# Attention maps mixed by ScalarE and GpSimd in place of VectorE, and the residual input added by TensorE

## What is computed

```python
q, k, v = split(h @ w_qkv); q = partial_rope(rmsnorm(q)); k = partial_rope(rmsnorm(k))
s = jnp.einsum('mbhqd,mbhkd->mbhqk', q_blk, k) * scale      # two maps m per head
p = jax.nn.softmax(s, axis=-1)
a = p[0] - lam * p[1]
o = jnp.einsum('bhqk,bhkv->bhqv', a, v)
o = rmsnorm(o, sub_gain) * (1.0 - lambda_init)
x = x + o @ w_o
```

## Time and profile before

| | us |
|---|---|
| median of 3 runs | 985.96 (985.76 to 987.13) |
| profiled execution, its own time | 985.77 |
| its span in the trace | 984.0 |
| TensorE busy | 971.3 (99%) |
| VectorE busy | 851.8 (87%) |
| ScalarE busy | 458.5 (47%) |
| GpSimd busy | 354.4 (36%) |

### The profile page before, as it was taken

The page is one execution under the profiler, slowest core; times in us unless marked ns, Lnnn a source line. Parts: engine busy times, 40 slices in busy tenths (PEclk is TensorE's granted clock), DMA queues, the critical chain, the costliest instruction groups (busy, mean ns, idle before and its releaser), DMA issues.

```text
span 984.0 us, 12869 instructions
## 1 busy us (share of the span) xinstructions
PE 971.3 (99%) x4706; PEld 799.2 (81%) x4706; DVE 851.8 (87%) x1132; ACT 458.5 (47%) x703; POOL 354.4 (36%) x317
## 2 busy tenths in 40 slices
PE   8999999989999999999999999999999999999998
PEld 7877778767887888888888888988888888888887
DVE  6696898999688999999989888779998989989883
ACT  5435555656556353443535533475355253452520
POOL 6841454121164638366543100550430403405000
PEclk9999999999999999999999999999999999999999
DMA  7242220120242233332333241303342332422202
GB/s 263 87 107 86 65 68 19 65 108 22 65 171 86 86 114 100 115 100 86 119 95 125 68 158 36 129 1 129 86 128 86 103 111 85 129 86 86 86 1 86
DMA packets 51543, 92.24 MB, mean 94 GB/s; under 512 B 8332, under 2 KB 9368, under 8 KB 51480
## 3 DMA queue, kind: packets, MB, share of 16 engines
q1 hardware_dynamic: 46032, 91.24, 29.0%
q10 hardware_dynamic: 5448, 0.17, 0.3%
HBM read 89.30 MB, written 2.10 MB: 93 GB/s over the span
## 4 chain that ended last, share of the span: by engine, by line
PE 70%; DVE 1%; ACT 0%; issue 0%; DVEq 0%; ACTq 0%
PE pair L1704 35%; PE bank L1704 34%; DVE s_acc L1543 0%; PE bank L2058 0%; DVE s_acc L1581 0%; PE pair L2046 0%; DVE s_hT_lo L1427 0%; DVE s_xT L1585 0%; DVE s_zn_lo L1650 0%; PE pair L2065 0%; ACT s_hT_hi L1034 0%; DVE s_u_raw L1445 0%; DVE s_u_lo L1563 0%; ACT s_u_hi L1124 0%; ACT s_u_raw L1054 0%
## 5 line engine op out<-in xcount | busy, mean ns | idle before, releaser
L789 POOL TENSOR_TENSOR s_lt<-s_lbB,s_lbB 128x1024 f32<-128x1024 f32 x14 | 33.6, 2400 | 259.4 <-PE pair L1704 162.8
L1220 DVE TENSOR_TENSOR s_lbB_lo<-s_lbB,s_b_hi 128x1024 fp32r<-128x1024 f32 x64 | 125.4, 1982 | 0.1
L1193 DVE TENSOR_TENSOR s_w_lo<-s_raw,s_w_hi 128x1024 fp32r<-128x1024 f32 x72 | 120.0, 1685 | 5.0 <-ACT s_w_hi L868 5.0
L890 ACT ACTIVATE s_b_hi<-s_lbB 128x1024 fp32r<-128x1024 f32 x64 | 67.2, 1053 | 80.3 <-POOL s_lbB L789 38.1
L1704 PE MATMUL bank<-s_hT_hi,s_w_hi 128*128 128x512 f32 x256 | 100.2, 392 | 0.0
L1704 PE MATMUL pair<-s_hT_hi,s_w_hi 128*128 128x512 f32 x256 | 100.1, 391 | 0.0
L1704 PE MATMUL bank<-s_hT_hi,s_w_lo 128*128 128x512 f32 x256 | 99.6, 389 | 0.0
L1704 PE MATMUL pair<-s_hT_hi,s_w_lo 128*128 128x512 f32 x256 | 99.6, 389 | 0.0
L1704 PE MATMUL bank<-s_hT_lo,s_w_hi 128*128 128x512 f32 x256 | 99.6, 389 | 0.0
L1704 PE MATMUL pair<-s_hT_lo,s_w_hi 128*128 128x512 f32 x256 | 99.6, 389 | 0.0
L1054 ACT ACTIVATE s_u_raw<-s_u_raw 128x512 f32<-128x512 f32 x64 | 40.4, 632 | 110.6 <-DVE s_u_raw L1445 110.6
(11 more groups left out here) (268 smaller groups left out, 2672.9 us busy)
## 6 DMA issues: line engine op xcount, KB each, us to landing
s_raw<-in_mlp_w SPq DMA_DIRECT2D x64, 512.0 KB, 3.7
s_lbB<-in_mlp_w SPq DMA_DIRECT2D x64, 512.0 KB, 3.3
s_raw<-in_attn_w_qkv SPq DMA_DIRECT2D x24, 512.0 KB, 3.9
s_raw<-in_attn_w_o SPq DMA_DIRECT2D x8, 512.0 KB, 3.2
s_x_again<-in_x SPq DMA_DIRECT2D x4, 512.0 KB, 6.2
out<-s_acc SPq DMA_DIRECT2D x8, 256.0 KB, 2.0
s_x_nat<-in_x SPq DMA_DIRECT2D x3, 512.0 KB, 8.0
s_raw<-in_pool_w SPq DMA_DIRECT2D x4, 256.0 KB, 2.8
```

The source lines that it names most:

```text
L789: g.tensor_tensor(w2_raw[n][:], w2_raw[one][:], w2_raw[two][:], ALU.subtract).then_inc(t_done, 1)
L890: a.activation(b_hi[home][:], w2_raw[n][:], ACT.Copy).then_inc(w2_hi_done, 1)
L1193: v.tensor_tensor(w_lo[slot][:, cols], raw[k][:], f32(w_hi[slot][:, cols]), ALU.subtract)\
L1220: v.tensor_tensor(w2_lo[n][:], w2_raw[n][:], f32(b_hi[home][:]), ALU.subtract).then_inc(w2_lo_done, 1)
```

## The change

Four things are changed.

1. The map is mixed by two engines. ScalarE multiplies the second map in place by the factor (`scaled`), between `keep_turn("map", i - 2)` and `exps(i)`; GpSimd adds it to the first (`combine`). VectorE now forms the factor ahead of the maxima.
2. Each map's maximum is a reduction of its own, and each exponential waits for its own maximum. The low part of q and k is made after the maxima; that of o stays ahead of them.
3. x is no longer loaded again, transposed and added by VectorE. TensorE adds it inside the sum of each `w_o` chunk by two products with an identity matrix, one with the high and one with the low part of the transposed input that is still there. `y_part` takes the place of `hT_hi`, chunk by chunk. `W_O_PARTS` and `SPLIT` get new steps, and one more part of the `w_o` product is done in the loop.
4. At the start the first 128 tokens come in one transfer and not in two halves, `keep_turning(4)` is `keep_turning(2)`, and the low part of the first q is made one tile earlier.

```diff
 W_O_PARTS = (
-    ((19, (0, 1, 2)), (21, (3,))),
...
+    ((20, (0, 1)), (21, (2, 3))),
...
-SPLIT = {4: (0, 1, 2, 3), 5: (5, 6, 7, 8), 6: (13, 14, 15, 19), 7: (27, 28, 29, 33), 8: (34, 34, 35, 35)}
+SPLIT = {4: (0, 1, 2, 3), 5: (4, 6, 6, 8), 6: (13, 14, 15, 19), 7: (26, 29, 31, 32), 8: (34, 34, 35, 35)}
...
-            sp.dma_start(x_nat[:, 0, 0:BANK], xv[:, 0, 0:BANK]).then_inc(x0_half_loaded, 16)
             for t in range(NT):
-                if t:
-                    sp.dma_start(x_nat[:, t, :], xv[:, t, :]).then_inc(x_loaded[t], 16)
+                sp.dma_start(x_nat[:, t, :], xv[:, t, :]).then_inc(x_loaded[t], 16)
                 sp.dma_start(raw[t][:].rearrange("p (a b) -> p a b", a=2), piece(0, t)).then_inc(raw_loaded[t], 16)
-                if t == 0:
-                    sp.dma_start(x_nat[:, 0, BANK:D], xv[:, 0, BANK:D]).then_inc(x_loaded[0], 16)
...
-            wait_used(sp, WO0 - 1)
-            for t in range(NT):
-                sp.dma_start(x_again[:, t, :], xv[:, t, :]).then_inc(x_again_loaded[t], 16)
...
+            def combine(i):
...
+                q = i % 2
+                pool.wait_ge(scaled, i + 1)
+                g.tensor_tensor(probs[q][:, 0, :], probs[q][:, 0, :], probs[q][:, 1, :], ALU.add).then_inc(a_done, 1)
...
             def exps(i):
-                act.wait_ge(max_done, i + 1)
                 if i >= 2:
                     act.wait_ge(turned, i - 1)
                 for m in range(2):
+                    act.wait_ge(max_done, 2 * i + m + 1)
                     a.activation(probs[i % 2][:, m, :], bank[m][:], ACT.Exp,
...
                 if 2 <= i < STEPS + 2:
                     keep_turn("map", i - 2)
+                if 1 <= i <= STEPS:
+                    q = (i - 1) % 2
+                    act.wait_ge(mix_known, i)
+                    a.activation(probs[q][:, 1, :], probs[q][:, 1, :], ACT.Copy, scale=mixc[:, q, :]).then_inc(scaled, 1)
                 if i < STEPS:
                     exps(i)
...
-                    if n == 2 * NT + 1:
+                    if n == 2 * NT:
                         turn_lo("q", 0)
...
-                v.tensor_reduce(nmax[:, i % 2, :], pair[0][:], AX.X, ALU.max, negate=True).then_inc(max_done, 1)
+                for m in range(2):
+                    v.tensor_reduce(nmax[:, i % 2, m:m + 1], bank[m][:], AX.X, ALU.max, negate=True).then_inc(max_done, 1)
...
-                v.scalar_tensor_tensor(probs[q][:, 0, :], probs[q][:, 1, :], mixc[:, q, :], probs[q][:, 0, :],
-                                       ALU.mult, ALU.add).then_inc(a_done, 1)
...
-                        v.tensor_tensor(y_part[:, c, :], y_part[:, c, :], bank[6 + f % 2][:], ALU.add)\
-                            .then_inc(wo_added, 1)
...
-            keep_turning(4)
+            keep_turning(2)
...
+                    if part == 0:
...
+                        mm(dst[:], ident_r[:], hT_hi[:, c, :], start=True)
+                        mm(dst[:], ident_r[:], hT_lo[:, c, :])
```

More of the change, by code:

```diff
@@ L103, in filler_steps @@
     for f in range(F_Y, F_END):
-        what, c = y_filler(f)
-        at |= {(f, u): step for u, (step, _) in enumerate(W_O_PARTS[c])} if what == "w_o" else {(f, 0): X_TURNED[c]}
+        at |= {(f, u): step for u, (step, _) in enumerate(W_O_PARTS[f - F_Y])}
     return at
@@ L377, in build_trunk @@
         r_done = sem("r_done")
-        x_turned = sem("x_turned")
         y_kept = sem("y_kept")
-        x_again_loaded = [sem(f"x_again_loaded{k}") for k in range(NT)]
+        ident_ready = sem("ident_ready")
         x_in_turned = sem("x_in_turned")
@@ L401, in build_trunk @@
         mix_known = sem("mix_known")
+        scaled = sem("scaled")
         a_done = sem("a_done")
@@ L744, in _ @@
                         .then_inc(o_normed, 1)
+                if 1 <= i <= STEPS:
+                    combine(i - 1)
                 for f in range(F_V):
@@ L1361, in mix_factor @@
                 dve.wait_ge(mix_rooted, i + 1)
+                if i >= 2:
+                    dve.wait_ge(scaled, i - 1)
                 v.scalar_tensor_tensor(mixc[:, i % 2, :], lsum[:, i, 0:1], neg_lam[:, 0:1], rl1[:, i % 2:i % 2 + 1],
                                        ALU.mult, ALU.mult).then_inc(mix_known, 1)
-            def combine(i):
-                q = i % 2
-                dve.wait_ge(mix_known, i + 1)
-                v.scalar_tensor_tensor(probs[q][:, 0, :], probs[q][:, 1, :], mixc[:, q, :], probs[q][:, 0, :],
-                                       ALU.mult, ALU.add).then_inc(a_done, 1)
             for i in range(LAST + 1):
-                if i - 1 in EXTRA:
+                if i - 1 in EXTRA and EXTRA[i - 1][0] == "o":
                     turn_lo(*EXTRA[i - 1])
@@ L1377, in _ @@
                         v_lo_part(1, f - F_V, bank[6 + f % 2])
-                for f in range(F_Y, F_END):
-                    what, c = y_filler(f)
-                    if TAKE[f] == i and what == "x":
-                        dve.wait_ge(y_kept, c + 1)
-                        dve.wait_ge(x_turned, c + 1)
-                        v.tensor_tensor(y_part[:, c, :], y_part[:, c, :], bank[6 + f % 2][:], ALU.add)\
-                            .then_inc(wo_added, 1)
                 if i >= 5 and i % 2 and (i - 5) // 2 < 2 * NH:
@@ L1389, in _ @@
                     mix_root(i - 1)
+                if 1 <= i <= STEPS:
+                    mix_factor(i - 1)
                 if i < STEPS:
                     maxima(i)
-                if 1 <= i <= STEPS:
-                    mix_factor(i - 1)
+                if i - 1 in EXTRA and EXTRA[i - 1][0] != "o":
+                    turn_lo(*EXTRA[i - 1])
                 if 2 <= i < STEPS + 2:
                     turn_lo("map", i - 2)
-                if 1 <= i <= STEPS:
-                    combine(i - 1)
                 if i >= 7 and (i - 7) % NT == 0:
@@ L1715, in turn_in @@
             def turn_in(t):
+                pe.wait_ge(x_loaded[t], 16)
                 for half in range(2):
                     n = 2 * t + half
[L1718 to L1721 removed]
                     if n >= 4:
@@ L1859, in filler @@
                         pe.wait_ge(side_lo_done, SIDE_NO["o", k] + 1)
-                        last = w_o_part(dst, c, k, k == 0, k == W_O_DONE[c] - 1)
+                        last = w_o_part(dst, c, k, False, k == W_O_DONE[c] - 1)
                     if k == W_O_DONE[c] - 1:
                         last.then_inc(wo_ready, 1)
-                else:
-                    for t in range(NT):
-                        if c == 0:
-                            pe.wait_ge(x_again_loaded[t], 16)
-                        last = nc.tensor.transpose(dst[:, t * P:(t + 1) * P], x_again[:, t, c * P:(c + 1) * P], ident[:])
-                    last.then_inc(x_turned, 1)
             def w_o_part(dst, c, k, start, stop):
```

48 lines of the change are left out of this document (22 added, 26 removed).

## The result

| | before | after |
|---|---|---|
| median, us (both measured again, 20 runs each) | 986.35 | 987.84 |
| ratio, 95% interval | | 1.0014 (1.0008 to 1.0020) |
| profiled execution, its own time | 985.77 | 988.01 |
| its span | 984.0 | 986.3 |

A forecast was written before the change was run, and what follows sets the result against it. TensorE's work plus its gaps was taken as the bound, with ScalarE's order limiting light loop steps. Terms −1.4 − 0.9 − 0.4 + 0.6 = −2.1 gave 983.7 profiled, 983.9 median; range 982.0 to 987.5 us.

The forecast's parts named there:

- the sum: Whole kernel: −1.4 − 0.9 − 0.4 + 0.6 = −2.1 us, giving a median of 983.9.
- Everything behind step 30: After the attention loop's step 30: two products more and two last transposes of x less on TensorE, −0.4 us.
- Part 1: Before the loop: q's low part made earlier removes TensorE's wait to turn k, −1.41 us.
- Part 4, the start: Kernel start: an idle gap before 8.67 may delay TensorE's clock rise, +0.6 us, ends 0 and +1.7.
- Parts 2 and 3, the loop: Attention loop, steps 18 to 30: new mixing and filler table together take 59.9 against 60.83 us, −0.9.
- The ring: Light loop steps: ScalarE's order of copy, scaling and exponentials sets the limit, 4.25 us, between 4.1 and 4.4.
- the addition's place off the path: Loop: GpSimd's addition takes 1.04 us, ends before the turn needing it, slack 1.2, costed at nothing.
- the surcharges: Loop: three steps set longer for extra work ahead of scaling or on ScalarE: step 19 5.1, 21 4.45, 27 4.6 us.
- Part 3: x by identity products: TensorE loses 3.7 us of transposes and gains 3.7 of products, net nothing; fillers redistributed over steps.
- Part 2: Loop: mixing on ScalarE and GpSimd with separate maxima relieves VectorE of 0.74 us; ScalarE's order limits light steps at 4.25.
- factor late: Rival in the loop: ScalarE's scaling and exponentials wait for VectorE's factor, up to 990.3 us; chance 0.15.

The follow-up runs named there:

- e3: Kernel before with only q's low part made one tile earlier: 984.50 us, ratio 0.9984.
- e11: Kernel before with only the new start (first 128 tokens in one transfer, two keep-turning transposes), without q's low part: 985.45 us, ratio 0.9997.
- e14: Kernel before with q's low part one tile earlier and the new start, nothing else: 983.21 us, ratio 0.9972.
- e6: Changed kernel with VectorE's reduction for s_oc moved behind the factor: 985.65 us, ratio 0.9996.
- e15: Kernel before with only the identity products for x and the new tables: 987.56 us, ratio 1.0017.
- e4: Changed kernel with T2 and T4 held for VectorE's low parts of the next weights, and q's and k's low part ahead of the maxima: 988.45 us, ratio 1.0017.
- e8: Kernel before with only the mixing on ScalarE and GpSimd, separate maxima and VectorE's new order: 989.20 us, ratio 1.0028.
- e7: Changed kernel with the mixing undone, VectorE combining behind the turned map's low part, all else kept: 988.92 us, ratio 1.0027.
- e9: Changed kernel with one VectorE wait: B11's low part in the first MLP block made only after GpSimd's T3: 985.67 us, ratio 0.9996.
- e13: Changed kernel with s_oc's reduction behind the factor, B11's low part behind T3, T4 behind the next weights' first low part: 983.75 us, ratio 0.9977.
- e2: Kernel before with GpSimd's T2 and T4 held until VectorE made the next weights' first and second low parts: 989.31 us, ratio 1.0034.

## Why the prediction was wrong

Three steps of the sum failed. Everything behind step 30 stood at −0.4, and the first MLP block, for which there is no term, cost +3.37. Steps 18 to 30 stood at −0.9 and came out at +0.72, and steps 0 to 17, taken as unchanged, at +0.64. The start stood at +0.6 and gained. The behaviour behind the first, that passes of VectorE and GpSimd hold each other, was in the prediction, but it was applied to the new additions only.

**Part 1** held: −1.6 for −1.4, alone (e3) and in the change.

**Part 4, the start,** had the wrong sign. The second tile is turned at 7.21 and not at 8.67; I had kept 8.67, as if nothing in front of that transfer had changed. By the distance between products the clock rose between 10.68 and 11.38, a few tenths later than before (between 10.29 and 10.80; the record's granted clock is 1.00 in both). Five projection products ran at the lower level and not one, but they ran 1.5 us earlier:

```profile
4.64 1.97 PE L1707 MATMUL bank<-s_ident,s_x_nat 128*128 128x128 f32 x8 [0.70 <-DMA s_x_nat<-in_x]
...
7.21 1.96 PE L1707 MATMUL bank<-s_ident,s_x_nat 128*128 128x128 f32 x8
8.82 0.78 PE L1689 MATMUL pair<-s_w_hi,s_hT_hi 128*128 128x512 f32 x1
9.39 0.63 PE L1689 MATMUL pair<-s_w_hi,s_hT_lo 128*128 128x512 f32 x1
...
11.38 0.40 PE L1689 MATMUL pair<-s_w_hi,s_hT_hi 128*128 128x512 f32 x1
11.61 0.40 PE L1689 MATMUL pair<-s_w_lo,s_hT_hi 128*128 128x512 f32 x1
```

Over all profiles the third tile's first product stands at 13.4 to 15.8 with the old start (five kernels, mean 14.5) and at 12.3 to 14.5 with the new one (thirteen, mean 13.2). So the new start is worth about −1.3 in the mean, with as much spread between executions; the medians say −0.8 (e11) and −1.2 (e14 against e3).

**Parts 2 and 3, the loop,** came out at +0.72 for −0.9 in steps 18 to 30. The ring that I had set as the limit was right: 4.19 in steps 18, 21 and 24, for 4.25, 4.45 and 4.3. So was the addition's place off the path, though not its price: it took 1.27 to 1.38 us in most steps and up to 2.33, for 1.04. Two turns are marked as waiting 0.36 for it (149.30 and 205.31), no longer than the turn of step 18 stands without such a mark. The step that failed is the costing of the surcharges. Of the 1.65 missed, 0.81 is step 19, exactly the 1.03 less 0.22 by which the square held the factor (e6 took it back: 5.10, my own figure). 0.75 is step 28, where the turn of `o` waits 0.54 for GpSimd, whose root for that `o` takes 1.93; I had no term for it. 0.40 of it comes with the new tables and not with the mixing: step 28 takes 5.26 in e15, and e6 brought it to 5.34. 0.28 and 0.27 are steps 22 and 26, where the extra turn waits for the low part that moved behind the maxima (e4 removed that wait, and paid for it elsewhere); other steps differ by under 0.35, mostly to the good. The same two causes make the +0.64 of steps 0 to 17, which I had costed at nothing: 0.40 in step 10, 0.21 and 0.12 in steps 15 and 16.

My sum for this stretch also hid two terms of opposite sign. Part 3, "net nothing" by products, is −1.15 there (e15): it spreads the filler over bare steps. Part 2, with the new order of VectorE's list, is +2.4 on the old tables (e8) and +1.9 on the new ones (61.55 against 59.68 of e15). Of the 1.9, e6 took back 1.1 by order alone, so 0.8 is left. No run prices the move of the mixing apart from the order: with the new list, mixing on VectorE cost 1.6 more (e7).

**The rival "factor late"** was the right mechanism in the wrong place. I tested its rule against the new addition, which ends ahead of the next factor, and left the sum alone. It was the old square of `s_oc` that met the factor. The factor had met GpSimd's passes before the change too, but then it stood behind the maxima, and the exponentials did not wait for it; the change put ScalarE's whole list behind it.

**The first MLP block** was no term at all, and is the largest: +3.37. Part 3 turns the order there (e15; e3, e8 and e11 do not). GpSimd's T1 begins 8.25 us after the first MLP product before, and 8.93 after, while VectorE's statistic, ahead of B11's low part, comes at 11.19 and 11.18. The rows show where the 0.68 us come from. Behind the loop TensorE does what is left of the `w_o` product, up to the first MLP product. Before:

```profile
277.83 0.70 PE L1704 MATMUL pair<-s_oT,s_w_hi 128*128 128x512 f32 x2 [0.23 <-DVE s_oT L1305]
...
285.43 0.39 PE L1704 MATMUL pair<-s_hT_hi,s_w_hi 128*128 128x512 f32 x1
...
293.68 2.40 POOL L789 TENSOR_TENSOR s_lt<-s_lbB,s_lbB 128x1024 f32<-128x1024 f32 x1
```

And after:

```profile
277.33 0.70 PE L1689 MATMUL pair<-s_oT,s_w_hi 128*128 128x512 f32 x2 [0.24 <-DVE s_oT L1302]
...
284.25 0.39 PE L1689 MATMUL pair<-s_hT_hi,s_w_hi 128*128 128x512 f32 x1
...
293.18 2.38 POOL L781 TENSOR_TENSOR s_lt<-s_lbB,s_lbB 128x1024 f32<-128x1024 f32 x1
```

GpSimd's chain of norm sums hangs on the first of these products, and T1 stands 15.85 behind it in both. The first MLP product, behind which TensorE's product for the statistic has its fixed place, stands 7.60 behind it before and 6.92 after: three products of 0.23, those of the one more `w_o` part that the new table does in the loop. All kernels with the new tables have 6.9 there and all with the old ones 7.6. No run moved that part alone. At T3 0.36 of the 0.68 is left, on an engine with much idle time, and it decides which of two instructions under 0.2 us apart goes first. That order, and T4's, are the cause: two waits gave back 2.8 of 3.4 (e9, e13), and two waits on GpSimd brought 3.1 us of loss to the kernel before (e2).

The Trainium skill has this rule ("SBUF — State Buffer", "Who interferes with whom"): a VectorE instruction with two SBUF inputs contends with a GpSimd one that reads SBUF; the port pair they share is locked for the whole instruction, and who issues first decides who waits; reductions, and instructions with at most one SBUF input outside VectorE's 2-port modes, stay free. The rows agree: `s_w_lo` took 3.42 behind a sum and 1.21 alone, T3 3.36 and 2.40, the factor 1.03 and 0.22, while `s_u_raw`, which reads PSUM and one SBUF tile, kept 1.29 for two beside T4. By the rule alone I could have listed every such pair ahead of TensorE's tight places; I applied it only to instructions that the change adds.
